# A four-layer mixer block on one core: the last two output products of layers 1 to 3, split by token halves

## The chip, the cores and the metric

The kernel runs on one core of a Trainium2 chip. The time is device microseconds (us) of the whole program. Three runs of the kernel before took 1384.91, 1386.80 and 1386.88 us: median 1386.8 us.

## The reference, cut to what matters

Two networks run one after the other on 256 tokens of width 1024. The first has four layers (named a0, b0, c0, a1 in the kernel), the second two (d0, d1). The change touches only the end of the first three layers of the first network, and the start of the layer that follows each:

```python
        y = jnp.concatenate([branch, mem_out], axis=-1) * jax.nn.silu(gate)
        y = jnp.matmul(y.astype(h.dtype), w_out[i])          # (256 x 1280) @ (1280 x 1024)
        h = layer_norm(DEEPNORM_ALPHA * h + y.astype(h.dtype), ln_g[i], ln_b[i])
    # next layer: proj = jnp.matmul(h, w_in[...]);  in a1 also branch = fourier_mix(h)
```

The layer norm needs the sum and the squares of a whole row of 1024 features, so of one token's row nothing can be normalised before both of its 512-wide halves are complete. Tokens don't need each other for it.

## The kernel before, in words

**Tiles.** The 256 tokens are two halves of 128 rows (`b` = 0, 1; NB = 2). The 1024 output features are two halves of 512 columns (`n` = 0, 1). So the output of a layer lies in four PSUM banks, bank `2*n + b`. All products are done in three passes on values split in a rounded part and a remainder (`mm3`, L457 to L459: hi x hi, then the two cross terms).

**Weights.** They come in units of at most 1 MB, in one fixed order. SyncE loads a unit into one of three `w_raw` slots as soon as VectorE has split the unit three places ahead of it. ScalarE rounds it (`w_hi`, L1517), which needs the split slot of the unit three places ahead to be done with on TensorE. VectorE then subtracts (`w_lo`, L2020). Where on ScalarE's and VectorE's own queues this happens is fixed by calls: `round_weights(key, ahead)` and `weights(key, ahead)` (also inside `product(key, ahead)`) do all units up to `ahead` units behind the one that TensorE uses at `key`. In what follows A and B are the last two units of a layer's `w_out` (rows 512 to 1023 of it, column half 0 and 1), and C, D and E the next three units, which belong to the layer that follows.

**The end of a layer.** TensorE adds the products of unit A to bank 0, then bank 1, then those of B to bank 2, then bank 3 (`out_unit(..., 4, 4)`; 12 matmuls of 512 columns for a bank, called a quarter below). VectorE takes statistics of each bank (`bn_stats`, L2426), and after bank 2 and after bank 3 works out mean and scale of the token half (`row_norm`, a chain of ten small instructions, each waiting for the last, L2140 to L2143). ScalarE then writes normalised rows into `z` (an arena tile) from banks 0, 2 and 3 (`normal_rows`, L1553), VectorE from bank 1 (`normal_half`, L2147).

**Into the next layer.** TensorE transposes the rows of a token half in four pairs of 128x128 tiles (`turn_rows`, L574) into banks 4 to 7: pair `j` into bank 4 + j, key `("zt", b, j)`. For the first token half ScalarE scales them (L1566) and rounds them to `h_hi` (L1548), and VectorE subtracts to `h_lo` (L2107, `half_lo`). For the second half VectorE scales (L2119). The next layer's first two units C and D are used by token halves too (`chunk_by_halves`): C on half 0, then the transposes of half 1, then D on half 0, C on half 1, D on half 1. Layer a1 instead begins with the first stage of a Fourier transform, `spectrum`, with tables for which no unit is needed: four products (`f1`, g = 0 to 3) of each token half, into banks 0 to 3 for either half, with the transposes of half 1 behind the second. ScalarE copies the results of half 0 out (L1604, L1605), VectorE those of half 1 (L2197, L2198). Then comes the product `qm` with unit C, in bank 6.

Each engine runs its queue in the order in which it is written, and waits by semaphores that are counted by key (`Steps`). Nothing else sets the order.

Of the kernel before, what the change touches and what calls it, by code (L numbers as in the profile page):

```python
# [30 lines left out]
P = 128  # L31
S = 256
NB = S // P
# [109 lines left out]
def build(nc, A, out):  # L143
    _, n_kept = constants()
    with ExitStack() as ctx:
# [195 lines left out]
        def S_(at, n):  # L341
            return stat[:, at:at + n]
# [81 lines left out]


        def f1_bank(j, g, b):
            return 2 * (g % 3) + b if j == 0 else g

        A_GATE_BANK, A_SPECTRUM_BANK = (2, 5, 1, 2, 7), (0, 4, 6, 7)
        B_PAIRS = [("m", p) for p in range(2)] + [("h", p) for p in range(8)]  # L430
# [15 lines left out]
        def _(pe):  # L446
# [8 lines left out]
            def mm3(o, lhs, rhs, start, stop):  # L455

                nc.tensor.matmul(o, lhs[0], rhs[0], start=start, stop=False)  # L457
                nc.tensor.matmul(o, lhs[0], rhs[1], start=False, stop=False)  # L458
                return nc.tensor.matmul(o, lhs[1], rhs[0], start=False, stop=stop)  # L459
# [99 lines left out]
                        if b == NB - 1:  # L559
                            i.then_inc(product_done.sem, product_done.next((L, "zt", j)))  # L560

            def turn_rows(L, b):

                for j in range(4):
                    n_b = 4 + j
                    if b == 1 and j < 2:
                        pe.wait_ge(rows_normal_v.sem, rows_normal_v.at(L))
                    else:
                        pe.wait_ge(rows_normal.sem, rows_normal.at((L, b, j // 2)))
                    if n_b in left:  # L570
                        pe.wait_ge(*left[n_b])
                    left[n_b] = (tiles_scaled if b == 0 else tiles_read).after((L, "zt", b, j))
                    for k in (2 * j, 2 * j + 1):
                        i = nc.tensor.transpose(bank[n_b][:, k % 2 * P:(k % 2 + 1) * P], z[:, b, k * P:(k + 1) * P], ident)  # L574
                    i.then_inc(product_done.sem, product_done.next((L, "zt", b, j)))
# [38 lines left out]
            def residual(L, n, bs=range(NB)):  # L614

                for b in bs:
                    if 2 * n + b in left:
                        pe.wait_ge(*left[2 * n + b])
                    if n == 0 and b == 1:
                        left[2 * n + b] = rows_normal_v.after(L)  # L620
                    else:
                        left[2 * n + b] = rows_normal.after((L, b, n))
                    for j in range(4):
                        for part, h_part in enumerate(hT(4 * n + j, b)):
                            nc.tensor.matmul(bank[2 * n + b][:, j * P:(j + 1) * P], h_part, ident_r[:], start=j + part == 0, stop=False)

            def out_unit(L, i, n, k0, kts, bs=range(NB)):


                if bs[0] == 0:  # L630
                    open_unit[L, n, k0] = unit(rows_of(A["w_out"][i], k0 * P, kts, n * 512, 512))
                u, w = open_unit[L, n, k0]
                for b in bs:
                    for k in range(kts):
                        if n == 0 and b == 0 and k % 2 == 0:
                            pe.wait_ge(r_ready.sem, r_ready.at((L, (k0 + k) // 2)))
                        m = mm3(bank[2 * n + b][:, :], rT(k0 + k, b), [a[:, k, :] for a in w], False, k0 + k == 7)
                    if k0 == 4:
                        m.then_inc(product_done.sem, product_done.next((L, "wo", n, b)))
                    elif b == NB - 1:  # L640
                        m.then_inc(product_done.sem, product_done.next(("unit", u)))
                unit_done[u] = (L, "wo", n, NB - 1) if k0 == 4 else ("unit", u)
# [28 lines left out]
            for li, (kind, j) in enumerate(LAYERS):  # L671
# [8 lines left out]
                if kind == "a":  # L680
# [97 lines left out]
                    residual(L, 1)  # L778
                    out_unit(L, li, 1, 8, 2)
                    out_unit(L, li, 1, 0, 4)  # L780
                    out_unit(L, li, 0, 4, 4)
                    out_unit(L, li, 1, 4, 4)
                elif kind == "b":
                    w = A["w_in_b"][0]

# [131 lines left out]
                    residual(L, 1, (1,))  # L917
                    out_unit(L, li, 1, 8, 2, (1,))
                    out_unit(L, li, 1, 0, 4)
                    out_unit(L, li, 0, 4, 4)  # L920
                    out_unit(L, li, 1, 4, 4)
                else:
                    w = A["w_in_c"][0]

# [189 lines left out]
                    residual(L, 1, (1,))  # L1114
                    out_unit(L, li, 1, 8, 2, (1,))
                    out_unit(L, li, 1, 0, 4, (1,))
                    out_unit(L, li, 0, 4, 4)
                    out_unit(L, li, 1, 4, 4)
                if li < len(LAYERS) - 1:
                    for b in range(NB):  # L1120
                        for j in range(4):
                            h_ready.at((LAYER_NAMES[li + 1], b, j))
                    turn_rows(L, 0)
                else:
                    hidden_from_rows(L, 4)


# [382 lines left out]
        def _(act):  # L1510
# [45 lines left out]
            def hidden_halves_hi(L, nxt, gain, shift):  # L1556

                normal_rows(L, 0, 0)
                normal_rows(L, 0, 1)
                for j in range(4):  # L1560
                    if j == 2:
                        normal_rows(L, 1, 1)
                    act.wait_ge(product_done.sem, product_done.at((L, "zt", 0, j)))
                    for m in range(2):
                        k = 2 * j + m
                        ins = nc.scalar.activation(tile_slot(j)[:, m, :], bank[4 + j][:, m * P:(m + 1) * P], ACT.Identity,  # L1566
                                                   scale=gain[:, k:k + 1], bias=shift[:, k:k + 1])
                    ins.then_inc(tiles_scaled.sem, tiles_scaled.next((L, "zt", 0, j)))
                    half_hi(nxt, 0, j, tiles_scaled)
                for j in range(4):  # L1570
                    half_hi(nxt, 1, j, tiles_read)

# [21 lines left out]
            for li, (kind, j) in enumerate(LAYERS):  # L1594
# [233 lines left out]
                    act.wait_ge(gate_read.sem, gate_read.at((L, "gate", 3)))  # L1828
                    nc.scalar.activation(flat2(gate[:, 6:8, :]), flat2(gate[:, 6:8, :]), ACT.Silu).then_inc(gate_ready.sem, gate_ready.next((L, "late")))

                round_weights((L, "wo", 1, 0), SPLIT_SLOTS - 1)
                if li < len(LAYERS) - 1:
                    hidden_halves_hi(L, LAYER_NAMES[li + 1], *ln_cols(li + 1))
                else:
# [176 lines left out]
        def _(dve):  # L2011
# [90 lines left out]
            def hidden_halves(L, nxt, gain, shift):  # L2102

                def half_lo(b, j):
                    pair, cols = slice(2 * j, 2 * j + 2), slice(b * P, (b + 1) * P)
                    dve.wait_ge(h_rounded.sem, h_rounded.at((nxt, b, j)))
                    v.tensor_tensor(h_lo[:, pair, cols], tile_slot(j), h_hi[:, pair, cols].bitcast(F32), SUB).then_inc(h_ready.sem, h_ready.next((nxt, b, j)))  # L2107

                half_lo(0, 0)
                normal_half(L, bank[1][:, :])  # L2110
                for j in range(1, 4):
                    half_lo(0, j)
                for j in range(5):
                    if j < 4:
                        product((L, "zt", 1, j), 1)
                        dve.wait_ge(h_ready.sem, h_ready.at((nxt, 0, j)))
                        for m in range(2):
                            k = 2 * j + m
                            ins = v.tensor_scalar(tile_slot(j)[:, m, :], bank[4 + j][:, m * P:(m + 1) * P], gain[:, k:k + 1], shift[:, k:k + 1], MUL, ADD)  # L2119
                        ins.then_inc(tiles_read.sem, tiles_read.next((L, "zt", 1, j)))  # L2120
                    if j:
                        dve.wait_ge(tiles_read.sem, tiles_read.at((L, "zt", 1, j - 1)))
                        half_lo(1, j - 1)
                dve.wait_ge(h_ready.sem, h_ready.made)
# [11 lines left out]
            def row_norm(L, b, factor=1.0):  # L2136


                mean, var = S_(152 + 2 * b, 1), S_(153 + 2 * b, 1)
                link(v.bn_aggr(S_(152 + 2 * b, 2), S_(128 + 12 * b, 12)))  # L2140
                ts(S_(4 + b, 1), var, 2.0 ** 26, 1e-5 / factor ** 2 * 2.0 ** 26, MUL, ADD)
                link(rsqrt_col(S_(8 + b, 1), S_(4 + b, 1), S_(6 + b, 1)))
                v.scalar_tensor_tensor(S_(10 + b, 1), mean, -1.0, S_(8 + b, 1), MUL, MUL).then_inc(row_stats.sem, row_stats.next((L, b)))  # L2143

            def normal_half(L, src):

# [43 lines left out]
            for li, (kind, j) in enumerate(LAYERS):  # L2190
# [134 lines left out]
                else:  # L2325
# [94 lines left out]
                        if q == C_TAIL + 1:  # L2420
                            heads_out(2, (L, "ao", 2))
                    heads_out(3, (L, "ao", 3))
                for n in range(2):
                    for b in range(NB):
                        product((L, "wo", n, b))
                        link(v.bn_stats(S_(128 + 12 * b + 6 * n, 6), bank[2 * n + b][:, :]))  # L2426
                        if n == 1:
                            row_norm(L, b, factor=ALPHA)
                if li < len(LAYERS) - 1:
                    hidden_halves(L, LAYER_NAMES[li + 1], *ln_cols(li + 1))  # L2430
                else:
                    normal_half(L, bank[1][:, :])
                    dve.wait_ge(act_read.sem, act_read.at(("cols", "b")))
                    split_hidden(L, LAYER_NAMES[li + 1], 4, *ln_cols(li + 1), natural=True, next_gain=col("mix", 0))
# [366 lines left out]
```

## Time and profile before

| | us |
|---|---|
| median of three runs | 1386.8 |
| the profiled execution | 1383.89 |
| its span | 1382.1 |
| TensorE busy | 1288.1 (93%) |
| VectorE busy | 866.8 (63%) |
| ScalarE busy | 702.0 (51%) |
| granted TensorE clock, mean | 0.973 |

The profiled execution's own time is 1.8 us above its span. The three layer boundaries lie at about 127 to 146 us (a0 to b0), 279 to 299 us (b0 to c0) and 645 to 666 us (c0 to a1). "PEclk" is the clock that TensorE was granted, as a share of full speed: 1.00 is 2.4 GHz and 0.50 is 1.2 GHz. In a timeline, the bracket at a row's end is the time that the engine stood idle before it, and who ended that.

### The profile page before, as it was taken

How to read it: one execution, taken by the hardware profiler on the slowest of the kernel's cores; microseconds unless marked ns; L12 is line 12 of the kernel's file. 1: busy time of each engine (PE TensorE's matmuls, PEld its weight loads, DVE VectorE, ACT ScalarE, POOL GpSimd, SP SyncE). 2: the span in 40 equal slices, each digit the busy share in tenths (PEclk: the TensorE clock that was granted, in tenths of full speed). 3: DMA queues.
4: the chain of work that ended last, by engine and by line, in shares of the span. 5: the costliest groups of instructions: out<-in, count | busy, mean ns of one | idle time of the engine just before them, and what ended most of it. 6: DMA issues, size and time to landing. Idle time of an engine off the chain costs nothing. (4 is left out here: it accounts for less than half of the span.)

```text
span 1382.1 us, 19921 instructions
## 1 busy us (share of the span) xinstructions
PE 1288.1 (93%) x7972; PEld 1125.1 (81%) x7972; DVE 866.8 (63%) x1519; ACT 702.0 (51%) x1014; POOL 2.4 (0%) x8
## 2 busy tenths in 40 slices
PE   5998998989989999898898897999999997999997
PEld 5887787767878787787797896798988996899996
DVE  6645986576473756546446798666455887755545
ACT  3624577543456755464423666544443666544442
POOL 0000000000000000000000000000000000000000
PEclk9999999999999999998999899999999999999998
DMA  9415332435542434224025352465665452365561
GB/s 302 130 60 200 111 122 78 166 104 182 183 153 92 153 122 153 92 97 155 32 92 172 97 174 92 122 213 172 194 191 164 118 176 92 123 210 190 178 210 50
DMA packets 146914, 197.53 MB, mean 143 GB/s; under 512 B 4717, under 2 KB 102279, under 8 KB 146695
## 3 DMA queue, kind: packets, MB, share of 16 engines
q1 hardware_dynamic: 146694, 196.22, 44.0%
q8 instruction: 64, 1.05, 0.3%
q14 instruction: 28, 0.22, 0.0%
q0 software_dynamic: 128, 0.04, 0.0%
HBM read 195.20 MB, written 1.05 MB: 142 GB/s over the span
## 5 line engine op out<-in xcount | busy, mean ns | idle before, releaser
L2020 DVE TENSOR_TENSOR w_lo<-w_raw,w_hi 128x2048 fp32r<-128x2048 f32 (+5 forms) x190 | 413.4, 2183 | 162.6 <-ACT w_hi L1517 160.5
L1517 ACT ACTIVATE w_hi<-w_raw 128x2048 fp32r<-128x2048 f32 (+5 forms) x190 | 345.6, 1828 | 294.0 <-PE bank L459 283.4
L457 PE MATMUL bank<-h_hi,w_hi 128*128 128x256 f32 x976 | 282.4, 289 | 6.8 <-DVE split_t L2345 3.6
L458 PE MATMUL bank<-h_lo,w_hi 128*128 128x256 f32 x976 | 278.8, 286 | 0.0
L459 PE MATMUL bank<-h_hi,w_lo 128*128 128x256 f32 x976 | 278.6, 285 | 0.0
L457 PE MATMUL bank<-w_hi,r_hi 128*128 128x512 f32 (+3 forms) x536 | 207.9, 388 | 7.1 <-DVE r_lo L2659 4.2
L458 PE MATMUL bank<-w_lo,r_hi 128*128 128x512 f32 (+3 forms) x536 | 204.7, 382 | 0.0
L459 PE MATMUL bank<-w_hi,r_lo 128*128 128x512 f32 (+3 forms) x536 | 204.4, 381 | 0.0
L457 PEld LDWEIGHTS bank<-h_hi,w_hi 128*128 128x128 f32 x976 | 190.1, 195 | 12.2 <-issue 4.4
L458 PEld LDWEIGHTS bank<-h_lo,w_hi 128*128 128x128 f32 x976 | 190.1, 195 | 0.6
L459 PEld LDWEIGHTS bank<-h_hi,w_lo 128*128 128x128 f32 x976 | 189.9, 195 | 0.0
L457 PE MATMUL bank<-w_hi,h_hi 128*128 128x512 f32 (+3 forms) x464 | 180.5, 389 | 7.3 <-DVE split_t L2345 3.7
L459 PE MATMUL bank<-w_hi,h_lo 128*128 128x512 f32 (+3 forms) x464 | 176.6, 381 | 0.0
L458 PE MATMUL bank<-w_lo,h_hi 128*128 128x512 f32 (+3 forms) x464 | 176.6, 381 | 0.0
L457 PEld LDWEIGHTS bank<-w_hi,r_hi 128*128 128x128 f32 x536 | 101.1, 189 | 27.9 <-issue 4.2
L459 PEld LDWEIGHTS bank<-w_hi,r_lo 128*128 128x128 f32 x536 | 101.1, 189 | 19.5
L458 PEld LDWEIGHTS bank<-w_lo,r_hi 128*128 128x128 f32 x536 | 101.3, 189 | 17.6
L457 PEld LDWEIGHTS bank<-w_hi,h_hi 128*128 128x128 f32 x464 | 88.7, 191 | 26.7 <-DVE split_t L2345 5.4
L459 PEld LDWEIGHTS bank<-w_hi,h_lo 128*128 128x128 f32 x464 | 88.5, 191 | 15.1
L458 PEld LDWEIGHTS bank<-w_lo,h_hi 128*128 128x128 f32 x464 | 88.7, 191 | 13.8
L2034 DVE TENSOR_TENSOR split_t<-masked 128x512 f32<-128x512 f32 x32 | 22.1, 692 | 87.3 <-ACT r_hi L2002 87.3
L1528 ACT ACTIVATE probT<-bank 128x512 f32<-128x512 f32 (+1 forms) x76 | 40.4, 579 | 55.9 <-PE bank L540 55.7
(270 smaller groups left out, 1385.7 us busy)
## 6 DMA issues: line engine op xcount, KB each, us to landing
w_raw<-in_mlp_w SPq DMA_DIRECT2D x64, 1024.0 KB, 5.4
w_raw<-in_w_out SPq DMA_DIRECT2D x24, 1024.0 KB, 5.1
w_raw<-in_w_in_c SPq DMA_DIRECT2D x48, 512.0 KB, 4.5
w_raw<-in_w_in_c SPq DMA_DIRECT2D x18, 1024.0 KB, 5.1
w_raw<-in_w_in_a SPq DMA_DIRECT2D x12, 1024.0 KB, 5.7
w_raw<-in_w_in_b SPq DMA_DIRECT2D x12, 1024.0 KB, 5.2
w_raw<-in_w_in SPq DMA_DIRECT2D x8, 1024.0 KB, 5.3
w_raw<-in_w_out SPq DMA_DIRECT2D x8, 512.0 KB, 3.9
```

The source lines that it names most:

```text
L457: nc.tensor.matmul(o, lhs[0], rhs[0], start=start, stop=False)
L458: nc.tensor.matmul(o, lhs[0], rhs[1], start=False, stop=False)
L459: return nc.tensor.matmul(o, lhs[1], rhs[0], start=False, stop=stop)
L1517: nc.scalar.activation(w_hi[:, u % SPLIT_SLOTS, 0:kts * n], w_raw[:, u % RAW_SLOTS, 0:kts * n], ACT.Copy).then_inc(w_rounded.sem, w_rounde ...
L1528: nc.scalar.activation(dst, src, func, scale=scale, **args).then_inc(act_read.sem, act_read.next(key))
L2020: v.tensor_tensor(w_lo[:, s, 0:m], w_raw[:, u % RAW_SLOTS, 0:m], w_hi[:, s, 0:m].bitcast(F32), ALU.subtract)\
L2034: link(v.tensor_tensor(o, a, b, op))
```

## The change: what it does

At the end of a0, b0 and c0 the quarters stand in the order bank 0, bank 2, bank 1, bank 3: both column halves of the first 128 tokens come first. Unit B is thus needed one quarter earlier. The statistics follow the same order, VectorE writes the first token half's rows from bank 2 (L2123 of the changed kernel) while ScalarE writes those from bank 0, and ScalarE writes both parts of the second half's rows. The first two pairs of transposes of the first half are put into the middle of the last quarter, the other two behind it. VectorE scales pair 1 of the first half, ScalarE pairs 0, 2 and 3. Unit D is rounded and subtracted later: on ScalarE behind the rounding of pair 1, on VectorE behind the second half's `row_norm`; at c0 to a1 even behind all tiles of both halves. In a1 `spectrum` uses banks 4 to 7 for the second token half. The last layer, a1, ends as before.

```diff
         def f1_bank(j, g, b):
-            return 2 * (g % 3) + b if j == 0 else g
+            return 2 * (g % 3) + b if j == 0 else 4 * b + g
...
-            def turn_rows(L, b):
+            def turn_rows(L, b, js=range(4)):
...
-                    if b == 1 and j < 2:
+                    if b == 0 and j >= 2:
                         pe.wait_ge(rows_normal_v.sem, rows_normal_v.at(L))
...
-                    left[n_b] = (tiles_scaled if b == 0 else tiles_read).after((L, "zt", b, j))
+                    left[n_b] = (tiles_scaled if b == 0 and j != 1 else tiles_read).after((L, "zt", b, j))
...
                         m = mm3(bank[2 * n + b][:, :], rT(k0 + k, b), [a[:, k, :] for a in w], False, k0 + k == 7)
+                        if turned and k == 1:
+                            turn_rows(L, 0, (0, 1))
...
-                    out_unit(L, li, 0, 4, 4)
-                    out_unit(L, li, 1, 4, 4)
...
-                    turn_rows(L, 0)
+                    for n, b in ((0, 0), (1, 0), (0, 1), (1, 1)):
+                        out_unit(L, li, n, 4, 4, (b,), (n, b) == (1, 1))
+                    turn_rows(L, 0, (2, 3))
                 else:
+                    for n in range(2):
+                        out_unit(L, li, n, 4, 4)
...
                 normal_rows(L, 0, 0)
-                normal_rows(L, 0, 1)
-                for j in range(4):
-                    if j == 2:
+                for j in (0, 2, 3):
+                    if j == 3:
+                        normal_rows(L, 1, 0)
                         normal_rows(L, 1, 1)
...
                     half_hi(nxt, 0, j, tiles_scaled)
+                    if j == 0:
+                        half_hi(nxt, 0, 1, tiles_read)
+                        round_weights((L, "zt", 1, 0), 1)
...
-                round_weights((L, "wo", 1, 0), SPLIT_SLOTS - 1)
+                round_weights((L, "wo", 1, 0), 1 if li < len(LAYERS) - 1 else SPLIT_SLOTS - 1)
...
+                def scaled(b, j):
+                    product((L, "zt", b, j), 1)
+                    for m in range(2):
+                        k = 2 * j + m
+                        ins = v.tensor_scalar(tile_slot(j)[:, m, :], bank[4 + j][:, m * P:(m + 1) * P], gain[:, k:k + 1], shift[:, k:k + 1], MUL, ADD)
+                    ins.then_inc(tiles_read.sem, tiles_read.next((L, "zt", b, j)))
+
+                out_stats(L, 0, 0, SPLIT_SLOTS - 1)
+                out_stats(L, 1, 0, 1)
+                row_norm(L, 0, factor=ALPHA)
+                dve.wait_ge(row_stats.sem, row_stats.at((L, 0)))
+                v.tensor_scalar(z[:, 0, 512:], bank[2][:, :], S_(152, 1), S_(8, 1), SUB, MUL).then_inc(rows_normal_v.sem, rows_normal_v.next(L))
+                out_stats(L, 0, 1, 1)
+                scaled(0, 1)
                 half_lo(0, 0)
-                normal_half(L, bank[1][:, :])
-                for j in range(1, 4):
-                    half_lo(0, j)
+                half_lo(0, 1)
+                out_stats(L, 1, 1, 1)
+                row_norm(L, 1, factor=ALPHA)
+                weights((L, "zt", 1, 0), 1)
+                half_lo(0, 2)
+                half_lo(0, 3)
```

TensorE, the last quarter of a0 in the kernel before; `arena` is `z`, `const` the identity that transposes:

```order
L459 MATMUL bank3<-w_hi,r_lo 128x512
L574 MATMUL bank4<-const,arena 128x128 [waits out_read,rows_normal]
L574 MATMUL bank4<-const,arena 128x128
L574 MATMUL bank5<-const,arena 128x128 [waits gate_read,rows_normal]
L574 MATMUL bank5<-const,arena 128x128
L574 MATMUL bank6<-const,arena 128x128 [waits out_read,rows_normal]
L574 MATMUL bank6<-const,arena 128x128
L574 MATMUL bank7<-const,arena 128x128 [waits out_read,rows_normal]
L574 MATMUL bank7<-const,arena 128x128
```

The same place in the changed kernel:

```order
L459 MATMUL bank3<-w_hi,r_lo 128x512
L574 MATMUL bank4<-const,arena 128x128 [waits out_read,rows_normal]
L574 MATMUL bank4<-const,arena 128x128
L574 MATMUL bank5<-const,arena 128x128 [waits gate_read,rows_normal]
L574 MATMUL bank5<-const,arena 128x128
L457 MATMUL bank3<-w_hi,r_hi 128x512
L458 MATMUL bank3<-w_lo,r_hi 128x512
```

Before, all eight transposes stand behind the last product of bank 3. Now four stand between its sixth and seventh product.

VectorE, a0 to b0, before, from the statistics to the tiles of the second token half:

```order
L2426 BN_STATS stat<-bank3 128x6 [waits product_done]
L2140 BN_AGGR stat<-stat 128x2 [waits vector_step]
L2037 TENSOR_SCALAR stat<-stat 128x1 [waits vector_step] x2
L2040 SCALAR_TENSOR_TENSOR stat<-stat 128x1 [waits vector_step] x5
L2134 SCALAR_TENSOR_TENSOR stat<-stat 128x1 [waits vector_step]
L2143 SCALAR_TENSOR_TENSOR stat<-stat 128x1 [waits vector_step]
L2107 TENSOR_TENSOR h_lo<-split_t,h_hi 128x2x128 [waits h_rounded]
L2147 TENSOR_SCALAR arena<-bank1,stat 128x512
L2107 TENSOR_TENSOR h_lo<-split_t,h_hi 128x2x128 [waits h_rounded] x3
L2119 TENSOR_SCALAR split_t<-bank4,col_a 128x128 [waits h_ready,product_done]
```

The same in the changed kernel:

```order
L2164 BN_STATS stat<-bank3 128x6 [waits product_done]
L2156 BN_AGGR stat<-stat 128x2 [waits vector_step]
L2040 TENSOR_SCALAR stat<-stat 128x1 [waits vector_step] x2
L2043 SCALAR_TENSOR_TENSOR stat<-stat 128x1 [waits vector_step] x5
L2150 SCALAR_TENSOR_TENSOR stat<-stat 128x1 [waits vector_step]
L2159 SCALAR_TENSOR_TENSOR stat<-stat 128x1 [waits vector_step]
L2023 TENSOR_TENSOR w_lo<-w_raw,w_hi 128x2048 [waits w_rounded]
L2110 TENSOR_TENSOR h_lo<-split_t,h_hi 128x2x128 [waits h_rounded] x2
L2116 TENSOR_SCALAR split_t<-bank4,col_a 128x128 [waits product_done,h_ready]
```

The subtraction of unit D has moved from ahead of bank 2's statistics to this place; the first two `h_lo` and the row copy have moved ahead of bank 3's statistics.

ScalarE, c0 to a1, before, from the last `h_hi` to the copies of the Fourier stage:

```order
L1548 ACTIVATE h_hi<-split_t 128x2x128 [waits tiles_read] x4
L1517 ACTIVATE w_hi<-w_raw 128x2048 [waits product_done,w_loaded1]
L1604 ACTIVATE arena<-bank0 128x256 [waits product_done]
L1605 ACTIVATE arena<-bank0 128x256
```

The same in the changed kernel:

```order
L1548 ACTIVATE h_hi<-split_t 128x2x128 [waits tiles_read] x4
L1517 ACTIVATE w_hi<-w_raw 128x2048 [waits product_done,w_loaded0]
L1517 ACTIVATE w_hi<-w_raw 128x2048 [waits product_done,w_loaded1]
L1607 ACTIVATE arena<-bank0 128x256 [waits product_done]
L1608 ACTIVATE arena<-bank0 128x256
```

Units D and E are now rounded one behind the other here, where E stood alone; and on VectorE the subtraction of D now stands directly ahead of its first copy of the Fourier stage.

## Rows read from the trace of the kernel before

**Rows 1.** The page: span, busy times, loads of b0's weights (KB each, us to landing).

```profile
span 1382.1 us, 19921 instructions
PE 1288.1 (93%) x7972; PEld 1125.1 (81%) x7972; DVE 866.8 (63%) x1519; ACT 702.0 (51%) x1014; POOL 2.4 (0%) x8
...
w_raw<-in_w_in_b SPq DMA_DIRECT2D x12, 1024.0 KB, 5.2
```

**Rows 2.** Timeline of TensorE, a0 to b0: start, duration, engine, line, operation.

```profile
124.50 0.39 PE L457 MATMUL bank<-w_hi,r_hi 128*128 128x512 f32 x1
...
126.99 0.39 PE L459 MATMUL bank<-w_hi,r_lo 128*128 128x512 f32 x1
129.98 1.33 PE L574 MATMUL bank<-const,arena 128*128 128x128 f32 x8 [2.60 <-ACT arena L1553]
...
132.37 0.47 PE L457 MATMUL bank<-w_hi,h_hi 128*128 128x512 f32 x1 [0.96 <-DVE h_lo L2107]
...
136.77 1.03 PE L574 MATMUL bank<-const,arena 128*128 128x128 f32 x8
137.56 0.47 PE L457 MATMUL bank<-w_hi,h_hi 128*128 128x512 f32 x1
...
146.35 0.50 PE L457 MATMUL bank<-w_hi,h_hi 128*128 128x512 f32 x1 [0.33 <-DVE w_lo L2020]
```

**Rows 3.** Timeline of VectorE, a0 to b0.

```profile
126.27 0.69 DVE L2426 BATCH_NORM_STATS2 stat<-bank 128x6 f32<-128x512 f32 x1
...
132.13 0.81 DVE L2147 TENSOR_SCALAR arena<-bank,stat 128x512 f32<-128x512 f32 x1
132.92 0.43 DVE L2107 TENSOR_TENSOR h_lo<-split_t,h_hi 128x256 fp32r<-128x256 f32 x1
...
137.19 1.36 DVE L2119 TENSOR_SCALAR split_t<-bank,col_a 128x128 f32<-128x128 f32 x4 [0.88 <-PE bank L574]
...
144.00 2.29 DVE L2020 TENSOR_TENSOR w_lo<-w_raw,w_hi 128x2048 fp32r<-128x2048 f32 x1
```

**Rows 4.** Timeline of ScalarE, a0 to b0.

```profile
129.15 1.45 ACT L1553 ACTIVATE arena<-bank,stat 128x512 f32<-128x512 f32 x2 [5.20 <-DVE stat L2143]
130.49 0.81 ACT L1566 ACTIVATE split_t<-bank,col_a 128x128 f32<-128x128 f32 x2
131.33 0.42 ACT L1548 ACTIVATE h_hi<-split_t 128x256 fp32r<-128x256 f32 x1
```

**Rows 5.** Timeline of TensorE, b0 to c0.

```profile
282.31 1.78 PE L574 MATMUL bank<-const,arena 128*128 128x128 f32 x8 [2.60 <-ACT arena L1553]
284.70 0.76 PE L457 MATMUL bank<-w_hi,h_hi 128*128 128x512 f32 x1 [0.60 <-DVE h_lo L2107]
...
289.86 1.03 PE L574 MATMUL bank<-const,arena 128*128 128x128 f32 x8
...
302.75 0.50 PE L457 MATMUL bank<-w_hi,h_hi 128*128 128x512 f32 x1 [0.94 <-DVE split_t L2345]
```

**Rows 6.** Timeline of VectorE, b0 to c0.

```profile
290.27 1.37 DVE L2119 TENSOR_SCALAR split_t<-bank,col_a 128x128 f32<-128x128 f32 x4 [1.63 <-PE bank L574]
```

**Rows 7.** Timeline of TensorE, c0 to a1.

```profile
648.47 1.97 PE L574 MATMUL bank<-const,arena 128*128 128x128 f32 x8 [2.60 <-ACT arena L1553]
...
661.10 0.39 PE L457 MATMUL bank<-dft_hi,h_hi 128*128 128x258 f32 x1 [4.26 <-ACT arena L1605]
...
665.59 0.28 PE L457 MATMUL bank<-h_hi,w_hi 128*128 128x256 f32 x1
```

**Rows 8.** Timeline of VectorE, c0 to a1.

```profile
654.93 1.36 DVE L2119 TENSOR_SCALAR split_t<-bank,col_a 128x128 f32<-128x128 f32 x4
...
662.33 0.42 DVE L2197 COPY arena<-bank 128x256 f32<-128x256 f32 x1 [3.10 <-PE bank L459]
```

**Rows 9.** Timeline of ScalarE, c0 to a1.

```profile
658.61 1.90 ACT L1517 ACTIVATE w_hi<-w_raw 128x2048 fp32r<-128x2048 f32 x1
```

**Rows 10.** Window: stretch, length, busy PE, PEld, DVE, ACT, POOL, then PEclk, DMA, GB/s.

```profile
286.00:287.00 1.00, 1.00 (x4) 0.71 (x4) 0.00 (x0) 0.97 (x4) 0.00 (x0) 0.50 0.00 0
```

More of the change, by code:

```diff
@@ L560, in hidden_from_rows @@
                             i.then_inc(product_done.sem, product_done.next((L, "zt", j)))
-            def turn_rows(L, b):
-                for j in range(4):
+            def turn_rows(L, b, js=range(4)):
+                for j in js:
                     n_b = 4 + j
-                    if b == 1 and j < 2:
+                    if b == 0 and j >= 2:
                         pe.wait_ge(rows_normal_v.sem, rows_normal_v.at(L))
@@ L618, in residual @@
                         pe.wait_ge(*left[2 * n + b])
-                    if n == 0 and b == 1:
+                    if (n, b) == ((0, 1) if L == LAYER_NAMES[len(LAYERS) - 1] else (1, 0)):
                         left[2 * n + b] = rows_normal_v.after(L)
@@ L625, in residual, with out_unit @@
                             nc.tensor.matmul(bank[2 * n + b][:, j * P:(j + 1) * P], h_part, ident_r[:], start=j + part == 0, stop=False)
-            def out_unit(L, i, n, k0, kts, bs=range(NB)):
+            def out_unit(L, i, n, k0, kts, bs=range(NB), turned=False):
                 if bs[0] == 0:
@@ L919, in _ @@
                     out_unit(L, li, 1, 0, 4)
-                    out_unit(L, li, 0, 4, 4)
-                    out_unit(L, li, 1, 4, 4)
                 else:
@@ L1116, in _ @@
                     out_unit(L, li, 1, 0, 4, (1,))
-                    out_unit(L, li, 0, 4, 4)
-                    out_unit(L, li, 1, 4, 4)
                 if li < len(LAYERS) - 1:
@@ L1558, in hidden_halves_hi @@
                 normal_rows(L, 0, 0)
-                normal_rows(L, 0, 1)
-                for j in range(4):
-                    if j == 2:
+                for j in (0, 2, 3):
+                    if j == 3:
+                        normal_rows(L, 1, 0)
                         normal_rows(L, 1, 1)
@@ L2107, in half_lo @@
                     v.tensor_tensor(h_lo[:, pair, cols], tile_slot(j), h_hi[:, pair, cols].bitcast(F32), SUB).then_inc(h_ready.sem, h_ready.next((nxt, b, j)))
-                half_lo(0, 0)
-                normal_half(L, bank[1][:, :])
-                for j in range(1, 4):
-                    half_lo(0, j)
+                def scaled(b, j):
[11 more added lines that the diff above has]
+                scaled(0, 1)
+                half_lo(0, 0)
+                half_lo(0, 1)
[4 more added lines that the diff above has]
+                half_lo(0, 3)
                 for j in range(5):
                     if j < 4:
-                        product((L, "zt", 1, j), 1)
                         dve.wait_ge(h_ready.sem, h_ready.at((nxt, 0, j)))
[L2117 to L2120, printed above, removed]
+                        scaled(1, j)
                     if j:
@@ L2143, in row_norm, with out_stats @@
                 v.scalar_tensor_tensor(S_(10 + b, 1), mean, -1.0, S_(8 + b, 1), MUL, MUL).then_inc(row_stats.sem, row_stats.next((L, b)))
+            def out_stats(L, n, b, ahead):
+                product((L, "wo", n, b), ahead)
+                link(v.bn_stats(S_(128 + 12 * b + 6 * n, 6), bank[2 * n + b][:, :]))
             def normal_half(L, src):
@@ L2422, in _ @@
                     heads_out(3, (L, "ao", 3))
[L2423 to L2428, printed above, removed]
                 if li < len(LAYERS) - 1:
@@ L2431, in _ @@
                 else:
+                    for n in range(2):
+                        for b in range(NB):
+                            out_stats(L, n, b, SPLIT_SLOTS - 1)
+                            if n == 1:
+                                row_norm(L, b, factor=ALPHA)
                     normal_half(L, bank[1][:, :])
```

## The prediction

> **What bounds the kernel now.** I read the page first: TensorE is busy for 1288.1 of 1382.1 us [rows 1], so only what shortens TensorE's gaps, or its work at the low clock, can count. Then I read the timelines of TensorE, VectorE and ScalarE side by side at the three layer boundaries, because the change touches nothing else. At a0 to b0 the last product starts at 126.99, and the first of the next layer that does real work at 132.37 [rows 2]. In between TensorE waits 2.60 us for the first normalised row and 0.96 us for the first h_lo. The reader is to see which chain this is: statistics of bank 2, row_norm, rows. From the start of that bn_stats at 126.27 [rows 3] to ScalarE's first row at 129.15 [rows 4] pass 2.88 us, and 0.83 us more to the first transpose. Behind such a wait the clock is halved (PEclk 0.50, which is 1.2 GHz; shown for b0 to c0) [rows 10]: here the twelve products from 132.37 to 136.77 take 4.40 us, where a full-clock quarter takes 12 x 0.226 = 2.72 us (from 124.50 to 126.99 are eleven steps of 0.226) [rows 2]. So 1.7 us are lost there. At b0 to c0 the wait is the same 2.60 us and the twelve products take 5.16 us, 2.4 us lost [rows 5]. At c0 to a1 there is a second wait, 4.26 us at 661.10, since bank 0 is read late by ScalarE [rows 7].
>
> Farther on a second engine matters. At 146.35 TensorE waits for w_lo of unit E [rows 2], and from the tiles of the second half at 137.19 to that w_lo at 144.00 VectorE has its fixed list of work, 6.81 us [rows 3]. What the change gives TensorE at 132 counts only as far as VectorE gets to 137.19 earlier.
>
> **The change part by part, a0 to b0**, on the clock of the trace before. The quarters end (last start 126.99 + 0.39 = 127.38, less 2.72 each) at 119.22, 121.94, 124.66, 127.38.
>
> 1. Bank 2 is now complete at 121.94. Its bn_stats can start a tenth later, at 122.05, since VectorE has nothing else to do then. Plus 2.88: rows at 124.93; plus 0.83: transposes can start at 125.76.
> 2. TensorE comes to them after six products of the last quarter, 124.50 + 1.36 = 125.86. The margin is 0.1 us, so I cost this wait at nothing. If the cover is gone, the rest of the last quarter waits behind the transposes, one for one. Eight transposes cost 0.79 us (136.77 to 137.56) [rows 2], four 0.4. The last quarter's issue then ends at 127.6, the other four transposes at 128.0. The wait of 2.60 us is gone; the same eight transposes are paid as before.
> 3. VectorE: row part from bank 2, 0.81 to 125.74; bn_stats of bank 1, 0.69; tile pair 1 (two of the four scalings of 1.36) to 127.2. ScalarE's pair 0 starts at 126.3, and 0.84 + 0.42 later h_hi is there, 127.6 [rows 4]. Two h_lo of 0.43 [rows 3] end at 128.0 and 128.5. The first product of b0 starts at 128.1 instead of 132.37, at full clock since it follows products without a rest, and C on half 0 ends at 130.85.
> 4. What is late next: row_norm of the second half. bn_stats of bank 3 starts only when VectorE is free, 128.45 (the bank is full at 127.9); plus 2.88 gives rows at 131.3 and transposes at 132.15. A new wait of 1.3 us. It has 8 transposes, D and everything behind it in its queue. The transposes of pair 3 wait for more: bank 7 is free when ScalarE has scaled pair 3, and this stands behind both rows: 131.3 + 1.45 + 0.81 = 133.55.
> 5. Unit D's w_lo, moved from ahead of bank 2's statistics, now lies on VectorE from 131.2 to 133.5 (2.29, its w_hi long done), and ahead of h_lo pair 2 (to 133.95) and pair 3 (h_hi at 133.55 + 0.45 = 134.0, so to 134.45). D starts at about 133.9 instead of 137.56, and VectorE's tiles of the second half at 134.45 instead of 137.19: 2.7 us earlier.
> 6. From there VectorE's list is unchanged, so w_lo of E starts at 141.3 and TensorE gets E at 143.65. TensorE needs three quarters from 133.9, to 142.1, or to 143.8 with one fall of the clock of 1.7 us. Both about equal VectorE's 143.65. This boundary gives 2.7 us; the bounds are 1.8 (a fall of 2.4 us) and 3.0 (the 0.33 us wait goes as well).
>
> SyncE loads the unit three behind D when w_lo of D is done, 7 us later than before (133.5 instead of 126.35). It is rounded only after D is done with on TensorE, at 142 us. That leaves 8 us for a load that takes 5.2 [rows 1]; I cost it at nothing. If it were late, the delay would stand in front of that unit one for one.
>
> **b0 to c0** has the same rows 152.33 us later (282.31 [rows 5] against 129.98). VectorE starts its tiles of the second half at 134.45 + 152.33 = 286.8 instead of 290.27 [rows 6]: 3.5 us. TensorE starts D at 286.2, which was 0.78 behind 289.86, 290.64: 4.4 us earlier, 2.7 if the clock falls once more. The next wait of TensorE is 0.94 us at 302.75 for VectorE [rows 5], so the smaller loss of TensorE hides there, and VectorE's 3.5 us counts. Bounds 2.8 and 4.1.
>
> **c0 to a1** is 518.5 us behind a0 to b0 (648.47 [rows 7] against 129.98). VectorE has no w_lo of D in the way, but h_hi of pair 3 waits for the rows all the same: 134.0 + 518.5 = 652.5, h_lo 652.95, tiles of the second half 2.0 us earlier than 654.93 [rows 8]. The 4.26 us wait [rows 7] goes with the banks 4 to 7. But now the product qm needs bank 6 again, from which VectorE must have copied g = 2. Ahead of that stand: w_hi of D at 658.61 - 2.0 = 656.6, 1.90 long [rows 9]; w_lo of D to 660.8; three pairs of copies of 2 x 0.42 each [rows 8], to 663.3. So qm starts at 663.3, 2.3 us before today's 665.59. TensorE has rested some 5 us by then, and qm starts in the low clock. Each fall seen above costs 1.7 to 2.4 us, where today qm is already at full speed. Leaves 0.3 us; bounds -0.1 and 2.3 (no fall).
>
> TensorE transposes and products stand in one queue. Where a transposition in it waited 2.60 us, no product started [rows 2]. The Trainium skill says the same, and it speaks against this change: in "TensorE: Matmul & The Clock Gate", section "Part 2: What happens when you issue a matmul", weight loads may be pulled ahead but matmuls stay in program order. By it, rows that come x us late hold back half a quarter of products for x us. By the sum x is 0.
>
> **Sum.** 2.7 + 3.5 + 0.3 = 6.5 us. Nothing downstream is tied to absolute time: no weight load after the start is waited for by ScalarE in the list of waits. The profiled execution took 1383.9 us, of which the span 1382.1; it becomes 1377.4. It stood 2.9 us under the median of the runs, so against that median I predict 1386.8 - 6.5 = 1380.3 us.
>
> **The rivals.**
>
> *The clock stays up as well.* For it: the long rest at each first boundary is cut up. Then TensorE's own gains count wherever VectorE allows: 3.0 + 4.1 + 2.3 = 9.4 us, 1377.4. Against it: about 1.3 us and then two shorter rests are left in the same place, and the 5 us rest in a1. The skill's page named above, "What's actually happening", says the low clock is the default and activity lifts it. By that, fewer rests could give the 1.7 and 2.4 us back; the rows here show the low clock right behind each 2.60 us wait, which agrees.
>
> *The gain is swallowed.* Two rests per boundary keep the clock low for 2.4 us each, or the margin of 0.1 us is negative by a microsecond at each boundary. 1.8 + 2.8 - 0.1 = 4.5, less 3 x 1.0 = 1.5 us: 1385.3, within what can be told from no change.
>
> *Slower.* One mechanism: falls of the clock. Place: inside each boundary, at the new wait before the second half's transposes, at pair 3, and at qm. Each costs up to 2.4 us. The gain is gone when they cost 6.5 us more than I count, three falls in addition. Five in addition would cost 12: 1386.8 + 5.5 = 1392.3. For it: the low clock after every long wait. Against: the new rests are shorter than 2.60 us except one, and half of what TensorE loses there hides behind VectorE.
>
> *The change doesn't do what it says* can be excluded for the order. But that a boundary's gain doesn't reach the end would need a wait that doesn't move with it; I see none.
>
> **How the numbers follow.** Forecast (4 to 8 us gained) 0.58; clock up as well 0.16; gain swallowed 0.18; slower 0.08. A measurement of this kernel can tell about 0.2% (2.8 us) from no change, so faster means under 1384.0: the first two cases and a little over half of the third (its upper part, 3 to 4 us), 0.84. Same: 0.11. Slower 0.05, as part of the last case stays under 1389.6. The range for 8 in 10 reaches from beyond the second case, 1376.2, to the upper part of the third, 1384.6.
>
> **What would show it.** Right: the 2.60 us waits of the transposes for ScalarE gone at all three places; a new one of about 1.3 us (2.5 at c0 to a1) before the second half's transposes; D's first product 3.7 us (4.4) earlier; the 4.26 us wait gone and one of about 5 us in front of qm, waiting for VectorE's copies. Wrong: PEclk at 1.00 throughout the boundaries (more gained), or four transposes in the last quarter that wait (step 2), or w_lo of D before the h_lo that D needs costing more than 134.45 says, or a wait for a weight load.

## The result and the profile after

The changed kernel took 1374.63, 1372.79, 1375.98, 1377.68 and 1379.30 us: median 1375.98 against 1386.24 for five runs of the kernel before, ratio 0.9929 (95% interval 0.9908 to 0.9949). That is 10.3 us less, where 6.5 were forecast; the median lies 0.2 us below the stated range. Six more runs beside 23 of the kernel before gave 1373.65 against 1384.88, ratio 0.9936 (0.9911 to 0.9960). The profiled execution took 1377.68 us, 6.2 less than that of before.

The page of the changed kernel, its span, busy times and granted clock in 40 slices:

```profile
span 1375.9 us, 19921 instructions
PE 1283.6 (93%) x7972; PEld 1121.3 (81%) x7972; DVE 868.2 (63%) x1525; ACT 700.3 (51%) x1008; POOL 2.4 (0%) x8
...
PEclk9999999999999999999999999999999999999999
```

The waits of the transposes are about what was forecast. TensorE, a0 to b0; this execution is 0.55 us later than that of before when it gets here:

```profile
126.41 0.60 PE L574 MATMUL bank<-const,arena 128*128 128x128 f32 x4
...
128.23 0.60 PE L574 MATMUL bank<-const,arena 128*128 128x128 f32 x4
...
128.70 0.47 PE L457 MATMUL bank<-w_hi,h_hi 128*128 128x512 f32 x1
...
132.53 1.11 PE L574 MATMUL bank<-const,arena 128*128 128x128 f32 x6 [0.81 <-ACT arena L1553]
133.99 0.41 PE L574 MATMUL bank<-const,arena 128*128 128x128 f32 x2 [0.35 <-ACT split_t L1566]
134.34 0.47 PE L457 MATMUL bank<-w_hi,h_hi 128*128 128x512 f32 x1
...
143.82 0.50 PE L457 MATMUL bank<-w_hi,h_hi 128*128 128x512 f32 x1 [1.07 <-DVE w_lo L2023]
```

The 2.60 us wait [rows 2] is gone, with none in its place at 126.41. The new one before the second half's transposes is 0.81 us, and pair 3 waits 0.35 us for ScalarE's scaling, as in step 4. Less 0.55, D's first product starts at 133.79 instead of 137.56, 3.8 us earlier (3.7 forecast). At b0 to c0 the two waits are 0.86 and 0.36 us, and D starts 4.5 us earlier (4.4 forecast). VectorE at a0 to b0:

```profile
122.60 0.70 DVE L2164 BATCH_NORM_STATS2 stat<-bank 128x6 f32<-128x512 f32 x1 [0.60 <-PE bank L459]
...
128.80 0.69 DVE L2164 BATCH_NORM_STATS2 stat<-bank 128x6 f32<-128x512 f32 x1
...
131.57 2.28 DVE L2023 TENSOR_TENSOR w_lo<-w_raw,w_hi 128x2048 fp32r<-128x2048 f32 x1
133.78 0.98 DVE L2110 TENSOR_TENSOR h_lo<-split_t,h_hi 128x256 fp32r<-128x256 f32 x2
134.67 1.36 DVE L2116 TENSOR_SCALAR split_t<-bank,col_a 128x128 f32<-128x128 f32 x4
...
141.47 2.29 DVE L2023 TENSOR_TENSOR w_lo<-w_raw,w_hi 128x2048 fp32r<-128x2048 f32 x1
```

Less 0.55, the tiles of the second half start at 134.12 instead of 137.19, and w_lo of E at 140.92 instead of 144.00 [rows 3]: 3.1 us each. What stands in VectorE's list between the two is still 6.80 us long.

At c0 to a1 the wait has moved. TensorE:

```profile
644.25 0.39 PE L457 MATMUL bank<-dft_hi,h_hi 128*128 128x258 f32 x1 [2.87 <-ACT arena L1553]
...
656.53 0.58 PE L457 MATMUL bank<-h_hi,w_hi 128*128 128x256 f32 x1 [4.55 <-DVE arena L2219]
```

The first row is the wait that was forecast at 2.5 us in front of the second half's transposes. It is 2.87 us long and stands six matmuls ahead of those transposes: the second Fourier product writes bank 1, out of which ScalarE first has to write the second half's rows. The second row is qm. VectorE ahead of qm, and then ScalarE's rounding of D and E in one row; VectorE waits for the first of the two:

```profile
652.20 2.29 DVE L2023 TENSOR_TENSOR w_lo<-w_raw,w_hi 128x2048 fp32r<-128x2048 f32 x1 [1.38 <-ACT w_hi L1517]
654.41 0.42 DVE L2218 COPY arena<-bank 128x256 f32<-128x256 f32 x1
```

```profile
650.20 3.70 ACT L1517 ACTIVATE w_hi<-w_raw 128x2048 fp32r<-128x2048 f32 x2
```

The 4.26 us wait in front of the second half's Fourier products [rows 7] is gone, and 4.55 us stand in front of qm: rounding of D, subtraction of D, three pairs of copies. Behind it the clock is low (windows of TensorE: stretch, its length, PE busy with the matmuls, PEclk, DMA share, GB/s):

```profile
656.50:658.00 1.50, 1.47 (x7) 0.50 1.08 385
658.00:660.00 2.00, 2.00 (x11) 0.50 0.46 152
660.00:662.00 2.00, 2.00 (x11) 0.50 0.67 228
662.00:664.00 2.00, 2.00 (x17) 0.84 0.85 296
```

To say where the time went I call the start of bank 0's statistics at the end of a layer its mark, and measure the stretches between the marks of a0, b0, c0 and a1, here and in the experiments below (e1 to e7). The marks of before are at 120.76, 273.09, 637.46 and 745.90 us; those of after:

```profile
121.31 0.69 DVE L2164 BATCH_NORM_STATS2 stat<-bank 128x6 f32<-128x512 f32 x1
...
270.13 0.69 DVE L2164 BATCH_NORM_STATS2 stat<-bank 128x6 f32<-128x512 f32 x1
...
630.98 0.70 DVE L2164 BATCH_NORM_STATS2 stat<-bank 128x6 f32<-128x512 f32 x1 [0.47 <-PE bank L459]
...
739.61 0.69 DVE L2164 BATCH_NORM_STATS2 stat<-bank 128x6 f32<-128x512 f32 x1
```

| kernel (one profiled execution each) | up to a0's mark | a0 to b0, b0 | b0 to c0, c0 | c0 to a1, a1 | median of the runs, us |
|---|---|---|---|---|---|
| before | 120.8 | 152.3 | 364.4 | 108.4 | 1386.2; 1384.9 beside e1 to e4; 1384.4 beside e5 to e7 |
| after | 121.3 | 148.8 | 360.9 | 108.6 | 1376.0 |
| e1 (after again) | 121.1 | 148.8 | 357.7 | 106.5 | 1373.7 |
| e2 (banks only) | 122.4 | 154.2 | 361.7 | 104.8 | 1383.7 |
| e3 (D early in a1) | 121.0 | 148.8 | 358.6 | 102.3 | 1370.9 |
| e4 (transposes behind) | 120.6 | 150.2 | 361.6 | 109.1 | 1380.1 |
| e5 (before, waits filled) | 121.0 | 150.9 | 362.3 | 108.6 | 1381.3 |
| e6 (VectorE loaded) | 121.0 | 151.4 | 358.4 | 107.1 | 1376.1 |
| e7 (e3, qm's unit early) | 121.2 | 150.4 | 358.5 | 102.1 | 1371.5 |

The first two stretches gave 3.5 us each, the third -0.2, what follows differs by 0.1, and the start was 0.55 later: together the 6.2 us of the profile.

### The profile page after: what moved, and what is told of

Its sections match the earlier page's. It is cut to its first block and busy times, and to the rows that moved or that the text cites. A ratio compares the mean times of both kernels' runs of the same rounds, so it can differ in the third digit from the quotient of the medians.

```text
span 1375.9 us, 19921 instructions
## 1 busy us (share of the span) xinstructions
PE 1283.6 (93%) x7972; PEld 1121.3 (81%) x7972; DVE 868.2 (63%) x1525; ACT 700.3 (51%) x1008; POOL 2.4 (0%) x8
```

## The experiments

**e1: the changed kernel again.** No edit.

> The changed kernel once more, unchanged. In the profile of it the first two boundaries and their layers gave 3.5 us each and the third lost 0.2 us, because the product qm starts after a wait of 4.55 us at the low clock; that profiled execution took 1377.68 us. Theory (the clock varies from execution to execution, the order of work does not): the waits of TensorE stay within 0.2 us of those seen (0.8, 0.35, 1.07 at a0 to b0; 2.87 and 4.55 at c0 to a1), the medians lie at 1374 to 1378 us, and executions differ by up to 6 us, with the difference in the stretches at the low clock. Rival (the 10 us between the medians come from the order of the work alone): every execution within 1 us of the next, and the profile shows shorter waits than seen.

Measured: 1371.60 to 1376.88 us, median 1373.65, ratio 0.9936 (0.9911 to 0.9960). The waits at a0 to b0 are 0.79, 0.35 and 1.06 us, as before; at c0 to a1 2.87 and 3.49, so one of them is 1.06 us off, against the expectation. The order did not change: qm starts 16.0 us behind bank 3's statistics in the first profile and 16.1 in this one. But here TensorE ran at the low clock from 638.9 to 645.7 us, was busy longer with what stands ahead of the wait, and so waited less. The two profiles of this same kernel differ by 5.9 us in span, 3.2 of them in the stretch of c0: in the first the clock was low for 6.8 us at both 400 and 570 us, in this one for 3.4 us each. TensorE in the two windows, first profile, then e1:

```profile
399.00:407.00 8.00, 6.47 (x33) 0.57 0.40 131
570.00:578.00 8.00, 6.62 (x33) 0.57 0.38 145
```

```profile
399.00:407.00 8.00, 6.71 (x47) 0.79 0.42 133
570.00:578.00 8.00, 8.00 (x57) 0.79 0.15 58
```

At half the clock 3.4 us more at each place cost 1.7 us each. So a single profile can't tell 3 us of c0 from chance.

**e2: the banks of the Fourier stage alone, in the kernel before.**

```diff
-            return 2 * (g % 3) + b if j == 0 else g
+            return 2 * (g % 3) + b if j == 0 else 4 * b + g
```

> The kernel before with one edit: the Fourier stage of a1 uses banks 4 to 7 for the second token half. Nothing else. Theory (the moved split of unit D costs what the banks gain): here D is split early as before, so VectorE copies as soon as each product is there; the wait of 4.26 us at 661.10 goes, the four products of half 1 run behind their h_lo to about 660, qm starts at about 661 instead of 665.6, no rest of 5 us precedes it. 3 to 5 us faster than before. Rival (ScalarE's late copies of half 0 or the h_lo chain set qm in any case): under 1 us.

Measured: median 1383.68 against 1384.88, ratio 1.0001 (0.9987 to 1.0016), so no change can be told, and the 3 to 5 us expected of the times did not show. The profile has the mechanism: the stretch of a1 is 104.8 instead of 108.4 us, with qm 24.3 us behind the mark (662.63 - 638.30) instead of 28.1 (3.8 us earlier, where about 4.6 were expected),

```profile
662.63 0.39 PE L457 MATMUL bank<-h_hi,w_hi 128*128 128x256 f32 x1 [1.00 <-DVE arena L2198]
```

while on unedited code the start was 1.6 us and the stretch of b0 1.9 us longer, with 6.8 instead of 3.4 us of low clock at 131 to 138, that of c0 2.7 us shorter, with 3.4 instead of 6.8 us of it at both 411 and 582, and what follows a1's mark 1.7 us longer. The mechanism is shown in the trace; that it makes the kernel faster is not shown by the times. What the change itself did in a1 is this gain less what moving D cost.

**e3: unit D split early at c0 to a1, in the changed kernel.**

```diff
+                    if j == 2 and L == "c0":
+                        round_weights((L, "zt", 1, 0), 2)
...
                 half_lo(0, 2)
+                if L == "c0":
+                    weights((L, "zt", 1, 0), 2)
                 half_lo(0, 3)
```

> The changed kernel, but at c0 to a1 unit D is rounded on ScalarE right behind h_hi of pair 2 (where ScalarE rests 1.77 us) and subtracted on VectorE right behind h_lo of pair 2 (where it rests 2.34 us). Theory (w_hi and w_lo of D, 1.9 + 2.3 us, are what qm waits for, and the rest brings the low clock): the wait of 4.55 us in front of qm falls to under 1 us, and qm runs at full clock; 4 to 6 us faster than the changed kernel, 1369 to 1372 us. Rival (the rest is set by ScalarE's copies or the chain of h_lo): at most 1 us faster than the changed kernel.

Measured: 1368.63 to 1371.56, median 1370.88, ratio 0.9909 (0.9888 to 0.9930): 2.8 us under the changed kernel run beside it (e1), and its slowest execution, 1371.56, is faster than the fastest of the changed kernel's eleven, 1371.60. VectorE, then TensorE, then TensorE's window from qm on:

```profile
640.82 2.29 DVE L2025 TENSOR_TENSOR w_lo<-w_raw,w_hi 128x2048 fp32r<-128x2048 f32 x1
643.23 0.42 DVE L2112 TENSOR_TENSOR h_lo<-split_t,h_hi 128x256 fp32r<-128x256 f32 x1
```

```profile
650.39 0.39 PE L457 MATMUL bank<-h_hi,w_hi 128*128 128x256 f32 x1 [0.98 <-DVE arena L2223]
```

```profile
650.00:656.00 6.00, 5.61 (x46) 1.00 0.26 83
```

The subtraction fits into VectorE's rest, qm waits 0.98 instead of 4.55 us, and PEclk is 1.00 from 650 to 656. The stretch of a1 is 102.3 us, 6.3 and 4.2 under the two profiles of the changed kernel. The theory holds; in the medians the gain is a little under the 4 us expected.

**e4: no transposes inside the last quarter, in the changed kernel.**

```diff
-                        out_unit(L, li, n, 4, 4, (b,), (n, b) == (1, 1))
-                    turn_rows(L, 0, (2, 3))
+                        out_unit(L, li, n, 4, 4, (b,))
+                    turn_rows(L, 0)
```

> The changed kernel, but all four pairs of transposes of the first token half stand behind the last quarter, none inside it. Theory (the margin in front of the transposes is about zero and they hold nothing back; what they feed, VectorE's tile pair 1 and the two h_lo ahead of bank 3's statistics, sets the second half's rows): everything behind comes 0.8 to 1.1 us later at each of the three boundaries, 2.5 to 3.3 us slower than the changed kernel. Rival (transposes inside the quarter hold back products and cost more than they bring): the same or up to 2 us faster than the changed kernel.

Measured: median 1380.06, ratio 0.9974 (0.9962 to 0.9986), 6.4 us slower than e1. VectorE in a0 to b0:

```profile
127.75 0.73 DVE L2116 TENSOR_SCALAR split_t<-bank,col_a 128x128 f32<-128x128 f32 x2 [1.57 <-PE bank L574]
...
129.42 0.69 DVE L2164 BATCH_NORM_STATS2 stat<-bank 128x6 f32<-128x512 f32 x1
```

VectorE waits 1.57 us for tile pair 1, and bank 3's statistics come 8.85 us behind the mark (129.42 - 120.57) instead of 7.49; at the other two boundaries they come 1.4 us later too. Of that the stretches keep 1.3, 0.7 and 0.4 us against the changed kernel's first profile, 2.5 in all, as expected. That is the fair pair, since both have the same low stretches from 157 us to a1's mark; against e1, which had less low clock in c0, the three stretches differ by 7.8. The rest of the 6.4 us between the medians I can't lay to a place. So the four transposes inside the quarter win 2.5 of the 6.2 us of the profile, and more by the medians; the sign is clear, the size is not.

**e5: the waits of the kernel before filled with matmuls that do nothing.**

```diff
+                    pe.wait_ge(*left[4])
+                    for _ in range(11):
+                        nc.tensor.matmul(bank[4][:, :], r_hi[:, 0, 0:P], r_hi[:, 0:2, :].rearrange("p a b -> p (a b)"), start=True, stop=True)
                     turn_rows(L, 0)
```

> The kernel before with 11 extra matmuls of 512 columns (into bank 4, whose content nobody reads; 11 x 0.226 = 2.5 us) between the last product and the first transposes at each of the three boundaries. They lie inside the wait of 2.60 us and change no wait or order. Theory (behind the wait the clock falls, and this is part of what the change won): PEclk stays 1.00 at the first two boundaries, the twelve products behind take 2.7 us instead of 4.4 and 5.2, VectorE's tiles of the second half come 0.9 us (its wait of 0.88 there) and 1.6 us (its wait of 1.63) earlier: the stretch from bank 0's statistics of a0 to those of b0 takes 151.4 us instead of 152.3 to 154.2, and the whole is 2 to 4 us faster than before. Rival (the low clock hides behind VectorE's list, or the extra matmuls don't hold the clock): within 1 us of before.

Measured: median 1381.29, ratio 0.9970 (0.9959 to 0.9982), 3.1 to 4.2 us faster than before, though nothing is computed earlier.

```profile
127.47 2.65 PE L1125 MATMUL bank<-r_hi 128*128 128x512 f32 x11
130.23 1.32 PE L574 MATMUL bank<-const,arena 128*128 128x128 f32 x8
...
135.42 1.03 PE L574 MATMUL bank<-const,arena 128*128 128x128 f32 x8
```

```profile
130.00:134.00 4.00, 2.92 (x16) 1.00 0.26 91
284.00:288.00 4.00, 4.00 (x23) 1.00 0.00 0
```

PEclk is 1.00 at both boundaries, where it was 0.50 at the second [rows 10] and, in this window of before, at the first:

```profile
133.00:136.00 3.00, 3.00 (x8) 0.50 0.00 0
```

From the first transposes to those of the second half pass 5.19 us instead of 6.79 (129.98 to 136.77) [rows 2]. Stretches: 150.9 and 362.3 instead of 152.3 and 364.4. The low stretches of c0 were 6.8 us long in both profiles, so the pair is a fair one. So a part of what the change wins in those two, 1.4 and 2.1 of 3.5 us each, is what the low clock had cost there. At c0 to a1 the same filling brought nothing (108.6 against 108.4): the wait in front of the second half's Fourier products, set by ScalarE's copies, grew from 4.26 to 4.98 us.

**e6: more work for VectorE at a0 to b0, in the changed kernel.**

```diff
+                if L == "a0":
+                    for _ in range(3):
+                        link(v.tensor_tensor(masked[:, 0, :], split_t[:, 0, :], split_t[:, 0, :], ADD))
```

> The changed kernel with three extra additions of 128x512 on VectorE (0.69 us each, 2.1 to 2.2 us with their waits, result not used) behind the last h_lo at a0 to b0 alone. Theory (behind the change VectorE's list sets when TensorE gets unit E, step 6 of the prediction): TensorE's wait for w_lo of E grows from 1.07 to 3.2 us, its later wait for w_lo (2.0 us) stays, and the stretch from bank 0's statistics of a0 to those of b0 grows from 148.8 to 151.0 us or more (a fall of the clock adds up to 1.7). Rival (TensorE's own work sets it, VectorE has slack): that stretch grows by under 1 us.

Measured: median 1376.10, ratio 0.9946 (0.9930 to 0.9962).

```profile
145.66 0.50 PE L457 MATMUL bank<-w_hi,h_hi 128*128 128x512 f32 x1 [3.23 <-DVE w_lo L2023]
...
158.85 0.36 PE L457 MATMUL bank<-h_hi,w_hi 128*128 128x256 f32 x1 [0.37 <-DVE w_lo L2023]
```

The wait for E is 3.23 instead of 1.07 us, ahead of any fall of the clock: all of VectorE's extra 2.2 us arrives there. The stretch is 151.4, 2.5 us longer; in it the clock fell elsewhere than in the changed kernel, so what goes beyond 2.2 us proves nothing. The median, 2.5 us above e1's and level with that of the first five runs, tells less than the trace. The later wait did not stay, it fell to 0.37, because a fall of the clock (147 to 151 us) now holds TensorE up in between. So VectorE's list sets when TensorE gets E, as step 6 said.

**e7: e3, and in b0 the unit of qm is subtracted 2.7 us earlier.**

```diff
                     for b in range(NB):
-                        weights((L, "p", 0, 0), 0)
+                        weights((L, "p", 0, 0), b)
                         rope_k(b)
```

> The changed kernel with unit D split early at c0 to a1 (1370.9 us when run alone) and one more edit: in b0 VectorE subtracts the unit of qm before it rotates the second half's keys, 2.7 us earlier. TensorE waits 2.01 us for this w_lo and then has a low clock for 3.4 us. Theory (this wait is only VectorE's order): the wait and the fall behind it go, 2.0 + 1.7 = 3.7 us, of which VectorE's chain to the first scores may take some back; the stretch from a0's to b0's statistics of bank 0 falls from 148.8 to 145 to 147 us, the whole to 1367 to 1369 us. Rival (VectorE is the bound all through b0's start, so TensorE just waits later, for the rotated keys or the maxima): no change, 148.8 us.

Measured: median 1371.48, ratio 0.9904 (0.9892 to 0.9917): as e3. The waits of TensorE from 143 to 195 us, in total, times and longest:

```profile
PE bank L457 <- DVE w_lo L2025: 4.9, 2, 3.8
```

The wait of 2.0 us is gone and one of 3.8 us stands before the next unit's w_lo, with the fall of the clock behind it instead (166 to 170 us); the stretch is 150.4 instead of 148.8. VectorE bounds the start of b0, and an order that serves one unit earlier lets TensorE wait for the next. The rival holds, and the stretch is even 1.6 us longer than it said. By their times e3 and e7 can't be told apart (0.9909 and 0.9904 of the kernel before); e3 is the simpler of the two best versions.

## Why the prediction was right, and where its sizes were off

**The bound** was read rightly: statistics, rows and transposes first, then VectorE's list. VectorE's tiles, predicted for 134.45 (in the times of before), came at 134.12.

**Steps 1 and 2** held to 0.2 us. The transposes in the last quarter found their rows and held nothing back. The Trainium skill's rule, matmuls in program order ("TensorE: Matmul & The Clock Gate", section "Part 2: What happens when you issue a matmul"), priced a lateness that did not occur. e4 shows what the place is worth.

**Steps 3 to 5** held in kind. The new wait was forecast as 1.3 us and is 0.81: in the times of before, the products of C reach until 131.2 instead of 130.85, and VectorE came 0.2 us earlier to bank 3's statistics. In the profile after, no engine waited for a weight load between 100 and 1200 us.

**Step 6** held in its mechanism (e6) and was mis-sized, 2.7 us where the trace has 3.1 at w_lo of E and 3.5 over the stretch. The first 0.3 is the chain, which reached VectorE's tiles that much earlier than forecast; then a later wait of VectorE for ScalarE, 0.33 us behind w_lo of E, went too. It also allowed for one more fall of the clock at each of the first two boundaries, hidden behind VectorE's list. None was seen there in any of the six profiles with the new order (after, e1, e3, e4, e6, e7; the fall of e6 at 147 us stands behind the wait that its edit lengthened). The order of before had low stretches of 3.4 and 6.8 us at the two boundaries in its own profile, and of 6.8 and 3.4 in e2's.

**b0 to c0**: 3.5 us predicted, 3.5 measured in the pair of profiles. That they are equal is luck: at VectorE's tiles the gain is 3.8 us, at TensorE's next wait (1.17 us instead of 0.94) 4.1, and e1's profile gives 6.7 over the stretch. **c0 to a1**: 0.3 us predicted, -0.2 in the pair, and 2.0 with e1's profile. The sum of the wait was right: qm came 25.55 us behind the mark instead of 28.13, 2.6 us earlier (2.3 predicted), and the low clock took 2.8 back (2.0 predicted). That it was the clock can be read from all nine profiles. From qm to a1's mark pass 80.3 to 80.4 us in the five without low clock behind qm's start (before, e2, e3, e5, e7), 81.7 with 2.9 us of it (e6), 81.9 with 3.4 (e1), 82.3 with 4.4 (e4) and 83.1 with 6.1 (after). In the traces e2 and e3 show that this place could have given 3.8 to 6 us: the banks are worth that, and the late split of D takes it.

**The sum** was 6.5, the pair of profiles gives 6.2, and the medians 10.3 and 11.2. The step that failed is the one from the profile to the median. It assumed that both kernels' medians stand at the same distance from their profiled executions. But that of before was 2.4 us under its median (1386.24), that of after 1.7 above its own: together the 4.1 us between 6.2 and 10.3. That 6.2 lies so near to 6.5 is partly luck, since e1's execution of the same kernel was 12.1 us faster than that of before. What differs between the two profiles of the changed kernel is mostly the low clock.

In the profile of before the clock was low for 54.6 us between 100 and 780 us, in that of after for 40.9, in e1's for 34.1. These sums don't turn into a gain by halving: e2's and e5's profiles had 41.0 us of it, 13.6 less than before, and took only 1.1 and 3.2 us less: other parts of these executions were longer, and low clock ahead of a wait for another engine need not cost time, as e5 shows at c0 to a1. The executions of one kernel spread over 7.7 us with the new order (1371.6 to 1379.3 us, eleven runs) and over 9.2 with the old (1377.5 to 1386.8, the 23 runs beside e1). The 3.4 us stretches in c0 also stand in e2's profile, with the old order. How much of the 4 us between profile and medians is a lasting effect of the new order, and how much the choice of the profiled executions, is not shown. I can't say what sets which wait is followed by a fall of 3.4 us and which by 6.8; that stays open.

Of the rivals, "swallowed" and "slower" rested on more falls of the clock; the new rests of 0.81 and 0.35 us brought none. "The clock stays up as well", given 0.16, was nearer to the medians than the forecast: it priced 9.4 us. Its sign, PEclk at 1.00 throughout, came true at the first two boundaries and not at c0 to a1, where the fall behind qm's rest came as forecast.

## What to carry to other kernels

Where a reduction over a row closes a stage, finish one half of the rows first and put its transposes into the products of the other half, at the point where their rows are just there: the place inside the last quarter was worth 2.5 of the 6.2 us that the profile gained. When such a reordering moves a shared chore (here the split of the next weights), look for the place where both engines rest: e3 won 2.8 us by that. Count what a wait costs with the clock behind it, and take several executions before crediting a few us to a stretch.

## What the runs showed of the hardware

Matmuls that do nothing, in the waits of 2.6 us at three boundaries, made the kernel 3 to 4 us faster (ratio 0.9970, 0.9959 to 0.9982): at the first two PEclk stayed at 1.00 (2.4 GHz) where it had fallen to 0.50 (1.2 GHz). The Trainium skill says that the low clock is the default and activity lifts it ("TensorE: Matmul & The Clock Gate", section "Part 1: The HAM clock gate (the "warmup" mystery)"); e5 agrees. Every low stretch between 100 and 740 us, in all nine profiles, was 3.4 or 6.8 us long, to 0.1 us; near 740 to 770 most were 10 to 14. Rests of 0.8 and 0.35 us close together brought no fall. Of the 17 single ones of 2.0 to 2.1 us before 740 us in the nine profiles, 14 had a fall at or just behind them: in the changed kernel's first profile the fall at 157 us stands behind such a rest, in e1 none stands behind the one at 625 us. That the low clock costs time is shown by e5 at the first two boundaries and by the way from qm to a1's mark in all nine profiles.
